# Trunk block on one core: the first two tiles of each perceptron take tokens before their norm is known

## The reference, cut to what matters

```
def rms_norm(x, g):
    return x * rsqrt(mean(x * x, axis=-1) + EPS) * g

def mlp(s, shift, scale_m):
    hm = rms_norm(s, g_norm2) * (1.0 + scale_m) + shift
    return square(relu(hm @ w_mlp1)) @ w_mlp2

x = x + gt1 * (y @ w_out)
x = x + gt2 * mlp(x, sh2, sc2)
```

## Time and profile before

| | |
|---|---|
| median of 3 runs | 2646.75 us (2645.33 to 2650.55) |
| the profiled execution's own time | 2643.97 us |
| its span | 2642.2 us |
| granted TensorE clock, mean | 0.98 |
| busy: TensorE, VectorE, ScalarE, GpSimd | 94%, 59%, 35%, 5% |

### The profile page before, as it was taken

One profiled execution on the slowest core, in us unless ns is written; L12 is line 12 of the kernel. 1 busy time (PEld: TensorE's weight loads), 2 busy tenths in 40 slices (PEclk: granted clock), 3 DMA queues, 4 the chain that ended last, 5 costly groups with the idle time before them and its releaser, 6 DMA issues.

```text
span 2642.2 us, 45632 instructions
## 1 busy us (share of the span) xinstructions
PE 2490.4 (94%) x19532; PEld 2028.9 (77%) x19532; DVE 1553.0 (59%) x2404; ACT 931.6 (35%) x1601; POOL 120.4 (5%) x230
## 2 busy tenths in 40 slices
PE   6999887789999999999999999999999998999997
PEld 3777666677877888877767888888887776788886
DVE  3555577757656888754674556544445466544444
ACT  3544433323235323332552422222223354422322
POOL 1000001111100000000000000000000000000000
PEclk8999899989999999999999999999999999999999
DMA  6100000014643555311002023333321102222210
GB/s 280 64 1 1 33 4 4 4 50 177 231 179 137 186 196 200 124 44 64 12 22 112 33 104 128 128 128 128 128 88 44 64 33 87 89 101 106 96 64 32
DMA packets 32201, 244.87 MB, mean 93 GB/s; under 512 B 3616, under 2 KB 3776, under 8 KB 20992
## 3 DMA queue, kind: packets, MB, share of 16 engines
q1 hardware_dynamic: 11808, 164.83, 15.6%
q0 software_dynamic: 20192, 77.11, 9.2%
HBM read 239.83 MB, written 2.10 MB: 92 GB/s over the span
## 4 chain that ended last, share of the span: by engine, by line
PE 87%; DVE 8%; issue 2%; ACT 2%; DMA 1%; POOL 0%; DVEq 0%; ACTq 0%; SPq 0%
PE ps L337 57%; PE ps L2239 2%; PE ps L2468 2%; PE ps L2496 1%; PE ps L997 1%; PE ps L2512 1%; PE ps L1419 1%; PE ps L367 1%; PE ps L2514 1%; PE ps L2513 1%; PE ps L368 1%; PE ps L369 1%; PE ps L953 1%; PE ps L999 1%; PE ps L998 1%
## 5 line engine op out<-in xcount | busy, mean ns | idle before, releaser
L337 PE MATMUL ps<-hh,ws 128*128 128x512 f32 x3168 | 735.9, 391 | 3.7 <-DVE xT L1856 3.1
L337 PEld LDWEIGHTS ps<-hh,ws 128*128 128x128 f32 x3168 | 591.7, 188 | 130.3 <-issue 8.1
L318 ACT ACTIVATE ws<-raw 128x1024 fp32r<-128x1024 f32 x295 | 308.9, 1049 | 431.8 <-PE ps L337 389.7
L326 DVE TENSOR_TENSOR ws<-raw,ws 128x1024 fp32r<-128x1024 f32 x295 | 359.6, 1220 | 164.4 <-ACT ws L318 164.4
L337 PE MATMUL ps<-g,ws 128*128 128x512 f32 x1536 | 355.3, 390 | 0.0
L337 PEld LDWEIGHTS ps<-g,ws 128*128 128x128 f32 x1536 | 286.3, 188 | 58.1
L337 PE MATMUL ps<-gg,ws 128*128 128x512 f32 x960 | 221.5, 391 | 2.1 <-ACT ws L318 2.1
L1856 DVE SCALAR_TENSOR_TENSOR xT<-ps,mods,xT 128x512 f32<-128x512 f32 x120 | 90.0, 750 | 212.8 <-PE ps L337 205.6
L337 PEld LDWEIGHTS ps<-gg,ws 128*128 128x128 f32 x960 | 181.2, 189 | 40.6 <-ACT ws L318 2.5
L2019 DVE TENSOR_TENSOR sq<-sq 128x512 f32<-128x512 f32 (+1 forms) x128 | 79.9, 624 | 140.4 <-ACT sq L1996 140.4
L1996 ACT ACTIVATE sq<-ps 128x512 f32<-128x512 f32 (+1 forms) x128 | 69.4, 542 | 252.4 <-PE ps L337 236.1
(11 more groups left out here) (385 smaller groups left out, 3610.4 us busy)
## 6 DMA issues: line engine op xcount, KB each, us to landing
raw<-in_w_m SPq DMA_DIRECT2D x32, 2048.0 KB, 7.8
raw<-in_w_ada POOLq DMA_DIRECT2D x80, 512.0 KB, 3.9
raw<-in_w_mlp SPq DMA_DIRECT2D x16, 2048.0 KB, 8.0
ar<-in_w_ada POOLq DMA_DIRECT2D x48, 512.0 KB, 3.9
raw<-in_w_in SPq DMA_DIRECT2D x8, 2048.0 KB, 7.6
raw<-in_w_mg SPq DMA_DIRECT2D x8, 1536.0 KB, 7.3
raw<-in_w_out SPq DMA_DIRECT2D x6, 2048.0 KB, 8.7
raw<-in_w SPq DMA_DIRECT2D x5, 2048.0 KB, 7.9
```

Of the source, the lines that this page charges most:

```text
L318: e.activation(w_of(n)[0], pieces[n][2], ACT.Copy).then_inc(*hi(n))
L326: e.tensor_tensor(l, pieces[n][2], h.bitcast(F32), ALU.subtract).then_inc(*lo(n))
L337: m = e.matmul(o, a, b, start=n == 0, stop=n == 3 * kt - 1)
```

## The change

Tiles 0 and 1 of x in each perceptron take z = x gain, split into its two parts, instead of the normed tokens. z is written into the hidden buffer while the out stage runs (`act_z`, `dve_z`). Their sums are multiplied by the root (`"scaled"`), and shift W is added as the bias of the relu (`SHIFT`): `dve_shift` multiplies the first two pieces by the shift and adds the eight feature blocks, `pe_shift` sums over partitions ahead of out tile 7, `dve_keep_shift` stores the result. The stat of x moves into the first `pe_tiles` of the perceptron, behind its feature blocks 0 and 1. There `ps.use` is 8 less the number of streams, then 8. Tile 2 waits for the normed blocks one by one and runs the context first. The split of piece 2 moves ahead of the norm. In the second block the norm's buffers for the context move to another place.

```diff
@@ pe_tiles
             for i, k in order:
+                if middle is not None and (i, k) == (0, 2):
+                    middle()
                 e.wait_ge(*dve[ready, k])
@@ new
+        SHIFT = mi[:, 8:10]
+        def act_z(e, tag, z, gain, m):
+            e.activation(z[:, 0, m, :], xT[:, m, :], ACT.Identity, scale=gain(m)).then_inc(*act((tag, "zhi", m)))
+        def dve_z(e, tag, z, gain, m):
+            e.wait_ge(*act[tag, "zhi", m])
+            e.scalar_tensor_tensor(z[:, 1, m, :], xT[:, m, :], gain(m), z[:, 0, m, :].bitcast(F32), ALU.mult,
+                                   ALU.subtract).then_inc(*dve(((tag, "z"), m)))
+        def dve_shift(e, tag, i, md, buf):
+            name, slot, w, _, _ = pieces[first[f"{tag}u0"] + i]
+            e.wait_ge(*raw_in[slot][name])
+            e.tensor_tensor(buf.rearrange("p (k c) -> p k c", k=KT), w, md[:, 24:32, 0:1].to_broadcast([P, KT, 128]),
+                            ALU.mult).then_inc(*dve())
+            for n in (512, 256, 128):
+                e.wait_ge(*dve.prev())
+                e.tensor_tensor(buf[:, 0:n], buf[:, 0:n], buf[:, n:2 * n], ALU.add).then_inc(*dve((tag, "part", i)))
+        def pe_shift(e, tag, bufs):
+            for t in ps.take((tag, "shift"), (7,)):
+                e.wait_ge(*t)
+            ps.n -= 1
+            for i in range(2):
+                e.wait_ge(*dve[tag, "part", i])
+                m = e.matmul(ps[tag, "shift"][:, 4 * i:4 * i + 4], bufs[i][:, 0:128], ones[:, 0:4], start=True, stop=True)
+            m.then_inc(*acc((tag, "shift")))
+        def dve_keep_shift(e, tag):
+            e.wait_ge(*acc[tag, "shift"])
+            e.tensor_copy(SHIFT, ps[tag, "shift"][:, 0:8].rearrange("p (i n) -> p i n", i=2)[:, :, 0]).then_inc(
+                *dve((tag, "shift")))
@@ tensor_out1, scalar_out1, vector_out1 (out2 of the second block alike)
             for m in range(8):
+                if m == 7:
+                    pe_shift(e, "m0", shift_1)
                 pe_tile(e, first["out0"] + m, [(("out", m), of(yy), T, "yy" if m == 0 else None)])
-            pe_stat(e, "x2", T, SQX, (7,))
...
                 act_square(e, "x2", m, xT[:, m, :], SQX)
+                act_z(e, "m0", gg, gain2, m)
...
                 dve_residual(e, ("out", m), xT, m, T, gate_col(mod, 2, m, 0))
+                if m:
+                    dve_z(e, "m0", gg, gain2, m - 1)
                 if 0 < m < KT - 1:
                     dve_square_sum(e, "x2", m, SQX)
+                if m in (4, 5):
+                    dve_shift(e, "m0", m - 4, mod, shift_1[m - 4])
+            dve_keep_shift(e, "m0")
@@ mlp_streams: tensor
-            def tensor(e, ready):
+            def tensor(e, ready, stat):
+                ps.use = range(8 - len(rows_))
-                for j, h, hid, x, w, bufs, bank in by_size:
+                for i, (j, h, hid, x, w, bufs, bank) in enumerate(by_size):
                     n = start("u", 0)
-                    pe_tiles(e, [n, n + 1], [(tag, "u", 0, m, j) for m in range(2)], of(h), w, by_feature, ready[j])
+                    pe_tiles(e, [n, n + 1], [(tag, "u", 0, m, j) for m in range(2)], of(h if j else hid), w, by_feature,
+                             ready[j] if j else (tag, "z"), middle=None if i else lambda: stat(e))
+                ps.use = range(8)
...
-                        pe_tile(e, start("u", q) + m, [((tag, "u", q, m, j), of(h), w, None)
-                                                       for j, h, hid, x, w, bufs, bank in rows_])
+                        early = q == 0 and m == 2
+                        pe_tile(e, start("u", q) + m, [((tag, "u", q, m, j), of(h), w, ready[j] if early else None)
+                                                       for j, h, hid, x, w, bufs, bank in (by_size if early else rows_)])
@@ mlp_streams: scalar
+                            if j == 0 and 8 * q + m < 2:
+                                e.wait_ge(*dve[tag, "scaled", m])
+                                e.activation(r, r, ACT.Relu, bias=SHIFT[:, m:m + 1]).then_inc(*act((tag, "u", q, m, j)))
+                            else:
+                                ...
@@ mlp_streams: vector
+                            if j == 0 and 8 * q + m < 2:
+                                e.wait_ge(*acc[tag, "u", 0, 1, 0])
+                                e.wait_ge(*dve.prev())
+                                e.tensor_tensor(r, ps[tag, "u", 0, m, 0][:, 0:w], rs[:, 0:w], ALU.mult).then_inc(
+                                    *dve((tag, "scaled", m)))
                             e.wait_ge(*act[tag, "u", q, m, j])
@@ scalar_mlp, vector_mlp (scalar_mlp0 and vector_mlp0 alike)
                     norm_c(range(0, 3))
+                split_hi(e, first[f"{mtag}u0"] + 2)
                 act_rms(e, (l, "so", 0), T, rs[:, :])
...
                 for j, h, hid, x, w, bufs, bank in out_rows[::-1]:
+                    if j == 0:
+                        dve_z(e, mtag, g2, gain2, 7)
+                        split_lo(e, first[f"{mtag}u0"] + 2)
                     dve_norm(e, (l, "mx", j), x, r_out[j], gains[j], shift2(md, j), h, bufs_m[j], (l, "so", j))
```

More of the change, by code:

```diff
@@ L355, in pe_tile, with pe_tiles @@
             acc.also(("used", n))
-        def pe_tiles(e, ns, names, rhs, w, order, ready):
+        def pe_tiles(e, ns, names, rhs, w, order, ready, middle=None):
             lhs = [pe_piece(e, n) for n in ns]
@@ L1864, in gate_col @@
             return md[:, part_ * 8 + mt, j:j + 1]
+        SHIFT = mi[:, 8:10]
[25 more added lines that the diff above has]
+                *dve((tag, "shift")))
+        shift_1 = [ar[:, 16384:17408], ar[:, 17408:18432]]
         def tensor_out1(e):
@@ L1991, in scalar @@
                             r = sq[:, (m + j) % 2, 0:w]
-                            e.wait_ge(*acc[tag, "u", q, m, j])
                             i = (8 * q + m) * len(rows_) + j
[L1994 to L1997, removed]
+                            if j == 0 and 8 * q + m < 2:
+                                e.wait_ge(*dve[tag, "scaled", m])
+                                e.activation(r, r, ACT.Relu, bias=SHIFT[:, m:m + 1]).then_inc(*act((tag, "u", q, m, j)))
+                            else:
+                                e.wait_ge(*acc[tag, "u", q, m, j])
+                                if i > 1:
+                                    e.wait_ge(*dve[tag, "r", i - 1])
+                                e.activation(r, ps[tag, "u", q, m, j][:, 0:w], ACT.Relu).then_inc(
+                                    *act((tag, "u", q, m, j)))
                             e.wait_ge(*dve[tag, "r2", i])
@@ L2122, in tensor_mlp0 @@
             ps.use = range(8)
-            mlp0[0](e, ["x2"])
+            mlp0[0](e, ["x2"], lambda e: pe_stat(e, "x2", T, SQX, (7,)))
         def scalar_mlp0(e):
+            split_hi(e, first["m0u0"] + 2)
             act_rms(e, "x2", T, rs[:, :])
@@ L2130, in vector_mlp0 @@
         def vector_mlp0(e):
+            dve_z(e, "m0", gg, gain2, 7)
+            split_lo(e, first["m0u0"] + 2)
             dve_norm(e, "x2", xT, rs[:, :], gain2, shift2(mod, 0), hh, bufs_2)
@@ L2167, in second @@
             out_rows = [(0, hh, None, xT, T, SQX, 7)] + ([] if last else [(1, hc2, None, ctx2, TC, SQC, 6)])
-            bufs_m = mod_bufs(T, ar2[:, 9216:10240]), [ar2[:, 256 * i:256 * i + 256] for i in range(4)]
+            bufs_m = mod_bufs(T, ar2[:, 9216:10240]), [ar2[:, 8192 + 256 * i:8448 + 256 * i] for i in range(4)]
+            shift_2 = [ar2[:, 9216:10240], ar2[:, 11264:12288]]
+            mtag = f"m{l + 1}"
             rows_ = [(0, hh, g2, xT, T, SQX, 7)] + ([] if last else [(1, hc2, gc2, ctx2, TC, SQC, 6)])
@@ L2761, in tensor_out2 @@
                     end = m == 7 and not last
+                    if m == 7:
+                        pe_shift(e, mtag, shift_2)
                     pe_tile(e, n + m, [((l, "out", m, j), of(h), w, None)
@@ L2774, in scalar_out2 @@
                         act_square(e, (l, "so", j), m, x[:, m, 0:w], bufs)
+                        if j == 0:
+                            act_z(e, mtag, g2, gain2, m)
             def vector_out2(e):
@@ L2782, in vector_out2 @@
                         dve_residual(e, (l, "out", m, j), x, m, w, gate_col(md, 2, m, j))
+                        if j == 0 and m:
+                            dve_z(e, mtag, g2, gain2, m - 1)
                         if 0 < m < KT - 1:
                             dve_square_sum(e, (l, "so", j), m, bufs)
+                    if m in (4, 5):
+                        dve_shift(e, mtag, m - 4, md, shift_2[m - 4])
+                dve_keep_shift(e, mtag)
             gains = lambda k: col(A2, k), lambda k: col(A2c, k)
@@ L2790, in tensor_mlp @@
                 ps.use = range(8)
-                up_down[0](e, [(l, "mx", 0), (l, "mx", 1)])
+                up_down[0](e, [(l, "mx", 0), (l, "mx", 1)], lambda e: pe_row_stat(e, (l, "so"), out_rows[0]))
             def scalar_mlp(e):
```

1 line of the change is left out of this document (removed).

## The result

The changed kernel takes 2664.32 us (median of 4 runs, 2659.31 to 2667.48), the kernel before, run beside it, 2648.65 us (median of 4, 2645.33 to 2650.87): a ratio of 1.0058, interval [1.0045, 1.0071]. It is slower by 15.7 us; 13.5 were forecast. The median stands 4.3 us above the 2660 that were forecast for it: 1.9 of that is the kernel before, whose median is higher here than the one shown, and 2.2 the change. That is inside the range of 2649 to 2665, but only 0.7 us from its end. The profiled execution took 2659.31 us, 2657.5 of it the span.

The account below looks back on a forecast made before the run. TensorE, busy 94% of the span, was taken as the bound. A 14.7 us loss in the second perceptron less gains of 0.15 and 1.05 gave 13.5 us longer: 2657.5 profiled, 2660 for a median, range 2649 to 2665.

Parts of the forecast that it names:

- The second perceptron: Perceptron with a context stream too: three steps lose 14.3 us, 14.7 with the shift; 9.6 if the clock stayed up.
- Step 1: Second perceptron: stat of x no longer fills the time before the context tiles; TensorE idles 4.7 us and the clock falls.
- Step 2: Second perceptron: root of x, waiting for its later stat, holds context copies 3 to 7; norm ends at 28.1, was 19.7.
- Step 3: Second perceptron: bank counter gives piece 2 the x tiles' banks, so it waits for their relus; piece 3 at 45.5, was 31.2.
- Rival B: Second perceptron: bank wait absent or short, loss there 5.2 + 0.4 us; sum 4.4 us longer, 2651; chance 0.12.
- One sign: Second perceptron: TensorE's granted clock was to show 0.50 three times.
- The first and third perceptron: One-stream perceptrons: earlier piece 3 gains 3.05 and 3.95 us, less clock 2.5 and shift 0.4: net 0.15 and 1.05.
- Its price: First and third perceptron: clock falls in the idle time before piece 3, adding 2.5 us at each.
- The shift: Ahead of out tile 7: two added shift matmuls of 4 columns on TensorE cost 0.4 us a place, 0.28 to 0.56.
- The work added to VectorE and ScalarE in the out stage: Out stage: tiles 4 and 5 run over by about 0.7 us each, tile 6 takes it back; costed at nothing.
- A: Rival: late pieces 3 and bank wait don't show; first and third gain 8.3 and 7.5 less 0.4; 2632 us; chance 0.09.
- C: Rival: clock stays up in the new gaps; second loses 9.6, others win at most 1.5 and 3.55; 2651 us; chance 0.07.

Follow-up runs that it names:

- the kernel with the conditioning spread: Changed kernel with x tiles first, bank counter stepped on, splits early, conditioning steps kept out of first-quarter up tiles, caught up over two quarters; 2632.51 us, ratio 0.9923 to before.
- the early splits alone: Changed kernel with pieces 3 and 4 split ahead of the relu of tile 0, first-quarter splits three ahead instead of two; ratio 1.0020 to the kernel before.

## Why the prediction was right

**The second perceptron** failed where it was said to, by the three steps, and the size was right: 14.7 us forecast, 14.1 measured. Part of that closeness is luck, since errors of the single steps cancel.
- Step 1, idle ahead of the context: 4.7 forecast, 4.73 measured, and the clock fell (0.68 in the 4.9 us behind it). It came back sooner than I had it: the granted clock is 1.00 again from 1478.2, 8.0 after zero, where I had the lower clock up to the stat's end at 10.9. So the root of x (its Exp) ends 11.1 after zero, forecast 12.35.
- Step 2, the root between context copies 2 and 3: seen as 3.88 us on ScalarE and 4.79 on VectorE. The norm of x ends at 26.8, forecast 28.1, for the reason just named. Moving the stat alone gave back 3.7 us of steps 1 and 2.
- Step 3, the banks: context half at 28.7 (29.5), x half at 36.8 (37.6), piece 3 at 44.9 (45.5). Stepping the counter alone gave back 8.5 us. From the norm's end to the x half it was 10.0 and not 9.5, which hid part of the error of step 2. The 48 matmuls from there took 2.6 us more than at full clock, forecast 2.5.

Rival B, and with it the lower end of the range, rested on a count made from the program. That count was the largest single risk. The one-number edit shows the clash that it gave, and `Banks.take` stepped through the whole program gives its numbers: 699 and 700, 702 and 703 in banks 3, 4, 0 and 1, then 704 and 705 in banks 0 and 1.

One sign was put wrong: the granted clock was to show 0.50 three times in the second perceptron. My own steps have two falls there, and the trace shows two (and one each in the first and the third perceptron).

**The first and third perceptron** gave 0.15 and 1.05 us in the forecast and -0.13 and 0.09 in the trace. Step by step: piece 3 started 23.8 after zero in the first (23.45 forecast) and 22.0 in the third (21.65). In both the norm ended at 16.7, as forecast; the chain behind it, from scaling to split, took 0.35 us longer than summed. The clock fell in both. Its price, by the 120 matmuls up to the first down tile, was 2.4 us in the first (29.90 us to their end, 27.52 before) and 3.0 in the third (30.17, where 120 times 0.227 is 27.2); I had 2.5 for both. The shift cost 0.36 a place up to the next matmul (784.19 to 784.55), and the 24 matmuls of out tile 7 behind it took 0.14 more than the other tiles (5.58 to the first z matmul at 790.13, where 24 times 0.227 is 5.45). That is 0.5 in all, forecast 0.4 from the lam row. The Trainium skill (VectorE: DVE Perf Modes, The TRN2 errata) gave an estimated 0.1 us for the four passes; the 0.36 measured speaks for the row and against that rule here. So the forecast of no gain in the first and little in the third held in mechanism. The third's gain was 1 us less than forecast: 0.4 at piece 3's start, 0.5 at the clock and 0.1 at the shift, all small.

**The work added to VectorE and ScalarE in the out stage** cost nothing on TensorE, as said: VectorE ran over by about 0.4 us in each of tiles 4 and 5 (0.7 forecast) and had taken it back by tile 7.

**The rivals.** A needed the relu and the split behind it before piece 2 ends: piece 3 waited 5.61 and 3.81 us. C needed the clock to stay up: it fell in all three places. I had set its bounds by two rows, a fall after 2.76 us of idle and none after 2.1. That is no rule: in the kernel with the conditioning spread, the up tile behind a wait of 1.93 us took 7.31 us in place of 5.60. What A promised does lie there, but only behind other work. The third perceptron gave it with the early splits alone: 7.0 us, where A had 7.1. The first gave 3.4 us at best in these runs and not 7.9, because the hidden units' chain, which no row of before showed as a limit (TensorE was later than it), takes the place of the split. I had named this chain only as far as piece 4.

**The 2.2 us between 13.5 and 15.7** are within what the runs scatter (the interval of the ratio is 12 to 19 us): the touched stages give 14.2 in the profiled pair, and the profiled executions differ by 15.3, of which 2.1 arose before the first out stage and -0.9 in the two stretches between.

## What to carry to other kernels

When work is freed of a wait, list what else stood behind that wait in program order, on every engine: here a weight split, a root and the relus all kept their place, and each became the next wait. A buffer handed out by a counter modulo the number in use changes its meaning when that number changes; it can turn two free buffers into two busy ones, and stepping the counter on was all that it took here. And a gain at the head of a pipeline lasts only as far as the slowest chain beside it can keep up: look at the rate of that chain per tile against TensorE's before counting the gain.

## What the runs showed that I had not expected

- The gain of an early start was given back in two perceptrons at the first down tile, 35 us later and more, by waits of 2.4 to 2.6 us. A loss of clock followed: the context half behind the one wait of 2.40 us took 4.52 in place of 3.04, and the 171 matmuls behind the two of 2.59 and 2.51 us took 2.4 us more. So these waits cost about one and a half times their length.
- A pass of 1.9 us on ScalarE at some of the first tiles is harmless only while TensorE is late too: 5.4 us a tile with it, 3.5 without, 7.1 with one on VectorE as well, against 5.45 on TensorE.
- The bank clash of the changed kernel has two small relatives in the kernel before: 1.0 us each at the last quarter of the first and of the third perceptron, where the number of banks in use goes from eight to seven. Reading all places where that number changes would have found them.
- Programs that are alike up to the first out stage reach it at 740.6 to 753.3 us in their profiled executions. That is as large as the whole effect of the change, so a single span can't judge it.
